# Second feed-forward matrix by seven half-size block products (Strassen) instead of eight

## The reference

```python
h = rmsnorm_2(x, mlp_norm[l])
u = jnp.square(jax.nn.relu(jnp.einsum('bsd,df->bsf', h, w_ff1[l])))   # 1024 -> 4096
x = x + jnp.einsum('bsf,fd->bsd', u, w_ff2[l])                        # 4096 -> 1024
```

## Time and profile before

| | before |
|---|---|
| median of 3 runs | 1589.47 us |
| profiled execution, its own time | 1590.67 us |
| span of that execution | 1588.9 us |
| TensorE, VectorE, ScalarE, GpSimd busy | 1547.0, 896.3, 697.8, 158.1 us |
| one feed-forward block | 87.1 us, eight of them |
| granted TensorE clock over the span | 0.997 of full speed |

### The profile page before, as it was taken

The page is one execution under the profiler, slowest core; times in us unless marked ns, Lnnn a source line. Parts: engine busy times, 40 slices in busy tenths (PEclk is TensorE's granted clock), DMA queues, the critical chain, the costliest instruction groups (busy, mean ns, idle before and its releaser), DMA issues.

```text
span 1588.9 us, 20931 instructions
## 1 busy us (share of the span) xinstructions
PE 1547.0 (97%) x7877; PEld 1263.9 (80%) x7877; DVE 896.3 (56%) x1498; ACT 697.8 (44%) x1185; POOL 158.1 (10%) x128
## 2 busy tenths in 40 slices
PE   7899999999999999999999999999999999999998
PEld 7676888877778788888888888778788888888886
DVE  5676557566866775534344345666876534344343
ACT  4355533545463774423223234563774423223232
POOL 3000222023000223000000002000223000000001
PEclk9999999999999999999999999999999999999999
DMA  5211232323211212233323232211212233233231
GB/s 171 71 33 54 80 107 80 106 95 105 80 54 62 71 55 82 95 102 107 98 87 106 79 106 89 97 52 55 66 55 91 81 106 104 89 99 106 79 106 53
DMA packets 127286, 135.62 MB, mean 85 GB/s; under 512 B 2458, under 2 KB 120804, under 8 KB 127204
## 3 DMA queue, kind: packets, MB, share of 16 engines
q1 hardware_dynamic: 126048, 133.18, 25.9%
q0 software_dynamic: 288, 1.05, 0.2%
q10 hardware_dynamic: 868, 0.31, 0.2%
HBM read 132.43 MB, written 2.10 MB: 85 GB/s over the span
## 4 chain that ended last, share of the span: by engine, by line
PE 81%; DVE 8%; ACT 4%; issue 4%; POOL 1%; DVEq 0%; ACTq 0%; POOLq 0%
PE U L1537 23%; PE U L1539 22%; PE U L1538 22%; PE U L1582 2%; PE U L1583 2%; PE U L1584 2%; PE Z L1715 1%; DVE pr L993 1%; PE Z L1730 1%; PE O L1782 1%; PE T L1755 1%; ACT tb L754 1%; PE O L1767 1%; PE Z L1641 1%; DVE WL L942 1%
## 5 line engine op out<-in xcount | busy, mean ns | idle before, releaser
L1537 PE MATMUL U<-XH,WL 128*128 128x512 f32 x976 | 386.4, 396 | 1.9 <-issue 1.9
L1539 PE MATMUL U<-XH,WH 128*128 128x512 f32 x976 | 380.5, 390 | 0.0
L1538 PE MATMUL U<-XL,WH 128*128 128x512 f32 x976 | 380.0, 389 | 0.0
L1537 PE MATMUL U<-MH,WL 128*128 128x512 f32 x848 | 336.8, 397 | 3.3 <-DVE tb L1398 1.7
L942 DVE TENSOR_TENSOR WL<-raw,WH 128x1024 fp32r<-128x1024 f32 x229 | 292.5, 1277 | 74.1 <-ACT WH L579 60.4
L579 ACT ACTIVATE WH<-raw 128x1024 fp32r<-128x1024 f32 x245 | 255.8, 1049 | 177.4 <-PE U L1539 171.1
L1539 PE MATMUL U<-MH,WH 128*128 128x512 f32 x848 | 330.6, 390 | 0.0
L1538 PE MATMUL U<-ML,WH 128*128 128x512 f32 x848 | 330.3, 389 | 0.0
L1537 PEld LDWEIGHTS U<-XH,WL 128*128 128x128 f32 x976 | 183.4, 188 | 45.0 <-issue 8.7
L1539 PEld LDWEIGHTS U<-XH,WH 128*128 128x128 f32 x976 | 183.2, 188 | 38.7
L1538 PEld LDWEIGHTS U<-XL,WH 128*128 128x128 f32 x976 | 183.6, 188 | 36.2 <-issue 0.2
(11 more groups left out here) (221 smaller groups left out, 1672.6 us busy)
## 6 DMA issues: line engine op xcount, KB each, us to landing
raw<-in_w_ff SPq DMA_DIRECT2D x64, 1024.0 KB, 5.3
raw<-in_w_in SPq DMA_DIRECT2D x24, 1024.0 KB, 5.1
raw<-in_attn_w_in SPq DMA_DIRECT2D x9, 1024.0 KB, 5.1
raw<-in_pool_w_in SPq DMA_DIRECT2D x8, 1024.0 KB, 5.4
raw<-in_w_o SPq DMA_DIRECT2D x8, 1024.0 KB, 5.0
raw<-in_attn_w_out SPq DMA_DIRECT2D x4, 1024.0 KB, 5.0
raw<-in_pool_w_out SPq DMA_DIRECT2D x4, 1024.0 KB, 4.9
xin<-in_x SPq DMA_DIRECT2D x2, 1024.0 KB, 6.4
```

The costliest lines, as they stand in the source:

```text
L1537: mm(o, wl, xh, start=first, stop=False, **kw)
L1538: mm(o, wh, xl, start=False, stop=False, **kw)
L1539: return mm(o, wh, xh, start=False, stop=last, **kw)
```

## The change

Only the second matrix changes. A pair of its output tiles (256 features), with 1024 hidden features and 512 tokens, is a product of 2 x 2 block matrices: weights in quarters (`quarters`: even or odd hidden tiles by left or right output tile), tokens in halves of 256 (B11, B21 the first halves of even and odd hidden tiles, B12, B22 the second). The variant of Strassen's scheme used makes seven products of 4 x 3 = 12 matmuls of 256 columns in place of eight. A block has four such pairs, q = 0 to 3, and a pair now is 85 matmuls: 83 of 256 columns and 2 of 512. Each engine's part:

- VectorE: four sums of weight quarters per pair (`corner_sums` 1024 wide for two of them, `third_sum`, `fourth_sum` 512 each) and their low parts (`sums_lo_of`, 1536 and 512 wide) beside the low parts of the three plain quarters (`first_halves_lo` 1024, `last_quarter_lo` 512). For the tokens, once per block: a 256-wide difference per hidden tile, two more per odd tile (`token_tile`), and per two tiles a 768-wide low part (`token_low`). The two 512-wide additions to `xT` per pair become five: `add_first` and `add_lower` 256 wide, `add_right`, `add_tops`, `add_bottoms` 512.
- ScalarE: the high parts of all these, and per pair two copies from PSUM to PSUM (`chain_copy`), which start partial sums in other banks.
- TensorE: `ff_pair`. It reads the hidden tiles k = 0, 2, 4, 6 first, then all odd ones, then the token sums. A pair may start when `add_right` of the pair before is done.
- New buffers lie over those of the attention part; `XH` of an even tile is now copied from `sq`, whose second half `token_tile` has replaced by a difference.

```diff
+                    for i in range(8):
+                        if i < 6:
                             conv(t0 + i + 2, b)
+                        elif i == 6:
+                            first_halves_hi(t0 + 8, b, (psum_done, b * 16 + (r0 + 6)))
+                            sums_hi_of(0, b, 0)
+                        else:
+                            sums_hi_of(0, b, 1)
+                            sums_hi_of(0, b, 2)
+                            last_quarter_hi(t0 + 8, b, r0 + 6)
                         if first and i == 0:
                             stat(plan["ff_stat", l])
-                        if i < 8:
-                            act.wait_ge(result_taken, b * 16 + (r0 + i + 1))
-                            a.activation(sq[:, i % 2, :], tb[:, i % 2, :], ACT.Square).then_inc(relu_squared, 1)
-                            a.activation(XH[:, i, :], tb[:, i % 2, :], ACT.Square).then_inc(second_hi_ready, 1)
-                        elif last:
-
-                            prep(G_ATTN + 8 * (l + 1) if l < DEPTH - 1 else None, i - 8, r0 + 16 * b + i, dst=MH)
+                        kp = i // 2
+                        act.wait_ge(result_taken, b * 16 + (r0 + i + 1))
+                        a.activation(sq[:, i % 2, :], tb[:, i % 2, :], ACT.Square).then_inc(relu_squared, 1)
+                        if i % 2 == 0:
+                            act.wait_ge(token_sums, b * 12 + (w0 + 3 * kp + 1))
+                            a.activation(XH[:, i, :], sq[:, 0, :], ACT.Copy).then_inc(second_hi_ready, 1)
+                        else:
+                            a.activation(XH[:, i, :], tb[:, 1, :], ACT.Square).then_inc(second_hi_ready, 1)
+                            act.wait_ge(token_sums, b * 12 + (w0 + 3 * kp + 3))
+                            a.activation(TH[:, kp, :], token_raw[:, kp, :], ACT.Copy).then_inc(token_hi, 1)
+                    for q in range(4):
+                        t = t0 + 8 + 2 * q
+                        chain_copy(q, b, 0)
+                        if q < 3:
+                            sums_hi_of(q + 1, b, 0)
+                            sums_hi_of(q + 1, b, 1)
+                            first_halves_hi(t + 2, b, (psum_done, b * 16 + (r0 + 8 + 2 * q)))
+                            chain_copy(q, b, 1)
+                            sums_hi_of(q + 1, b, 2)
+                            last_quarter_hi(t + 2, b, r0 + 8 + 2 * q)
+                        else:
+                            if not last or t + 16 * (BLOCKS - 1) + 2 < LAST_T:
+                                conv(t + 2, b)
+                            chain_copy(q, b, 1)
+                            if not last or t + 16 * (BLOCKS - 1) + 2 < LAST_T:
...
+                def chain_copy(q, b, i):
+
+                    p1, u, z, _ = strip(q)
+                    act.wait_ge(chain_done, b * 8 + (c0 + 2 * q + i + 1))
+                    if i == 0:
+                        dst, src = u, p1
+                    else:
+                        dst = z.rearrange("p (a h n) -> p a h n", a=2, h=2)[:, :, 1]
+                        src = u.unsqueeze(1).broadcast_to([P, 2, 256])
+                    a.activation(dst, src, ACT.Copy).then_inc(chain_copied, 1)
+
...
+                def corner_sums(q, b):
+
+                    t = t0 + 8 + 2 * q
+                    dve.wait_ge(raw_landed[t // 2 % 2], b * 64 + 16 * (t // 4 + 1))
+                    if q >= 2:
+                        dve.wait_ge(psum_done, b * 16 + (r0 + 8 + 2 * q - 2))
+                    shared = quarters(t)[:, 0, 1].unsqueeze(1).broadcast_to([P, 2, 4, P])
+                    out_ = sums_raw[:, q % 2, 0:1024].rearrange("p (j k c) -> p j k c", j=2, k=4)
+                    v.tensor_tensor(out_, corners(t), shared, ALU.subtract).then_inc(weight_sums, 1)
...
+                def token_tile(i, b):
+
+                    kp = i // 2
+                    c0, c1 = slice(0, 256), slice(256, 512)
+                    dve.wait_ge(relu_squared, b * 8 + (u0 + i + 1))
+                    if i % 2 == 0:
+                        v.tensor_tensor(sq[:, 0, c1], sq[:, 0, c0], sq[:, 0, c1], ALU.subtract).then_inc(token_sums, 1)
+                    else:
+                        v.tensor_tensor(token_raw[:, kp, c0], sq[:, 1, c1], sq[:, 0, c1], ALU.subtract).then_inc(token_sums, 1)
+                    dve.wait_ge(second_hi_ready, b * 8 + (m0 + i + 1))
+                    v.tensor_tensor(XL[:, i, :], sq[:, i % 2, :], XH[:, i, :].bitcast(F32), ALU.subtract).then_inc(second_ready, 1)
+                    if i % 2:
+                        dve.wait_ge(token_sums, b * 12 + (w0 + 3 * kp + 2))
+                        v.tensor_tensor(token_raw[:, kp, c1], sq[:, 1, c0], token_raw[:, kp, c0], ALU.subtract)
+                        v.scalar_tensor_tensor(out=token_raw[:, kp, 512:768], in0=token_raw[:, kp, c0], scalar=-1.0, in1=sq[:, 0, c0],
+                                               op0=ALU.mult, op1=ALU.subtract).then_inc(token_sums, 1)
+
+                def token_low(kp, b):
+
+                    dve.wait_ge(token_hi, b * 4 + (k0 + kp + 1))
+                    v.tensor_tensor(TL[:, kp, :], token_raw[:, kp, :], TH[:, kp, :].bitcast(F32), ALU.subtract).then_inc(token_lo, 1)
...
+                def add_right(q, b):
+
+                    _, _, _, e = strip(q)
+                    dve.wait_ge(fifth_done, b * 4 + (h0 + q + 1))
+                    right = xT[:, 2 * q:2 * q + 2, 256:512]
+                    v.tensor_tensor(right, right, e.unsqueeze(1).broadcast_to([P, 2, 256]), ALU.add).then_inc(half_added, 1)
...
+                    for i in range(8):
+                        if i < 6:
                             conv(t0 + i + 2, b)
+                        elif i == 6:
+                            first_halves_lo(0, b)
+                            fourth_sum(0, b)
+                        else:
+                            sums_lo_of(0, b, 0)
                         if first and i == 0:
                             stat(plan["ff_stat", l])
+                        if i in (2, 4, 6):
+                            token_low(i // 2 - 1, b)
                         ps = result(r0 + i, b)
-                        if i < 8:
-
-                            v.scalar_tensor_tensor(out=tb[:, i % 2, :], in0=ps, scalar=0.0, in1=rstd[:, 0:S], op0=ALU.max,
-                                                   op1=ALU.mult).then_inc(result_taken, 1)
-                            dve.wait_ge(relu_squared, b * 8 + (u0 + i + 1))
-                            dve.wait_ge(second_hi_ready, b * 8 + (m0 + i + 1))
-                            v.tensor_tensor(XL[:, i, :], sq[:, i % 2, :], XH[:, i, :].bitcast(F32), ALU.subtract).then_inc(second_ready, 1)
-                        else:
-                            kt = i - 8
-                            add_x(ps, kt, last, r0 + 16 * b + i if last else None)
-                            if last and l < DEPTH - 1:
-                                prep_lo(G_ATTN + 8 * (l + 1), kt, (MH, ML))
-                            elif last:
-                                v.tensor_scalar(xf[:, kt, :], xT[:, kt, :], gain[:, G_LAST + kt:G_LAST + kt + 1], None, ALU.mult).then_inc(xt_ready, 1)
+                        v.scalar_tensor_tensor(out=tb[:, i % 2, :], in0=ps, scalar=0.0, in1=rstd[:, 0:S], op0=ALU.max,
+                                               op1=ALU.mult).then_inc(result_taken, 1)
+                        if i == 5:
+                            corner_sums(0, b)
+                        token_tile(i, b)
+                        if i == 5:
+                            third_sum(0, b)
+                    sums_lo_of(0, b, 1)
+                    token_low(3, b)
+                    last_quarter_lo(0, b)
+                    for q in range(4):
+                        t = t0 + 8 + 2 * q
+                        if q < 3:
+                            corner_sums(q + 1, b)
+                        if q:
+                            add_lower(q - 1, b)
+                            add_tops(q - 1, b)
+                        if q < 3:
+                            third_sum(q + 1, b)
+                            fourth_sum(q + 1, b)
+                            sums_lo_of(q + 1, b, 0)
+                            first_halves_lo(q + 1, b)
+                        add_first(q, b)
+                        if q:
+                            add_bottoms(q - 1, b)
+                        if q < 3:
+                            sums_lo_of(q + 1, b, 1)
+                            last_quarter_lo(q + 1, b)
+                        elif not last or t + 16 * (BLOCKS - 1) + 2 < LAST_T:
+                            conv(t + 2, b)
+                            conv(t + 3, b)
+                        add_right(q, b)
+                        if last and q:
...
+                    if q >= 2:
+                        pe.wait_ge(result_taken, b * 16 + (r - 2))
+                    else:
+                        pe.wait_ge(result_taken, b * 16 + (r0 + 7))
+                    if q:
```

(28 more changed lines are left out.)

194 lines of the change are left out of this document (179 added, 15 removed).

## The result

The kernel after takes 1650.97 us, the median of 4 runs (1648.05 to 1651.53), beside 1589.33 us (1588.98 to 1591.76) for the kernel before. The ratio is 1.0379, 95% interval 1.0364 to 1.0395: slower, as forecast, and 12 us slower than the 1639 us forecast. The profiled execution took 1648.05 us with a span of 1646.2 us; that of before had 1588.9 us, so 57.3 us are to be accounted for.

A forecast was written before the change was run, and what follows sets the result against it. TensorE, busy 97% of the span, was taken as the bound, with VectorE falling late. Four blocks at +5.2 plus 2.8 a layer, two layers 47.2, +0.7 and +1.4 gave +49.3: 1639 us, with 8 in 10 from 1603 to 1666.

The forecast's parts named there:

- TensorE's gain, 0.47 us a pair: Second matrix: a pair of output tiles goes from 10.88 to 10.41 us, 14.9 us over 32 pairs.
- The first matrix falls behind: First matrix: the helpers' chain takes 11.8 us per two tiles against TensorE's 10.88; VectorE loses 0.9 us each time.
- The waits of pair 0, 7.1 us: Hand-over to the second matrix: six TensorE waits of 1.2, 1.9, 1.8, 0.9, 0.5, 0.7 us; pair 0 takes 17.5.
- So I add nothing: Hand-over: 3.4 us at half clock loses 1.7 us of matmuls, hidden by 2.1 us of waits; if later, 14 us more.
- Pairs 1 to 3 with 1.2 us of slack: Later pairs: VectorE needs 9.1 us against 10.41, so they run at TensorE's rate with 1.2 us to spare.
- Blocks of 92.3, first blocks 95.7: Feed-forward blocks: 92.3 us each, +5.2; a layer's block 0 a further +2.8 with small ends, forecast as 95.7.
- The layer change, +0.7: Between the layers: last rows of `xT` complete 1.1 and 2.2 us after TensorE's end, the norm's last sum late: +0.7 us.
- The end, +1.4: Very end: the last square starts 2.2 us after TensorE and ends at 2.9, where the norm's matmul was at 1.7: +1.4.
- From profiled to median: Whole program: the median lies 1.2 us below the profiled execution, so 1640.0 becomes 1639 us.
- The rival of the VectorE-bound pairs: Every pair: 0.1 us more on each of 12 VectorE instructions uses up the slack; 1675 us and up, chance 10%.
- the rule of the Trainium skill: VectorE: next instruction waits until the pipe is empty, 0.09 us more a step; 95.8 us a block, 1667 total, chance 3%.
- Vector keeps up: Rival in the first matrix: the waits hide and the kernel gets faster, 1577 us; chance 4%.

The follow-up runs named there:

- e5_reorder: Kernel after with the end-of-layer edits and the helpers' work in another order, each relu VectorE's first step for its tile, TensorE's order unchanged: 1605.94 us, ratio 1.0090.
- e8_small_acc: Kernel after with GpSimd's additions of the squares behind each layer's feed-forward done on 8 columns in place of 512: 1641.88 us, ratio 1.0316.
- e4_relu_early: Kernel after with the relus of tiles 6 and 7 put ahead of pair 0's weight work on VectorE: 1629.95 us, ratio 1.0243.

## Why the prediction was right, and where 12 us are missing

- **TensorE's gain, 0.47 us a pair.** Right: pairs of 10.39 and 10.40 us without idle time, and half columns cost +20.3 us for +19.7.
- **The first matrix falls behind.** Right: from the relu of tile 2 to that of tile 4 in the layer's first block, 651.99 to 663.85, are 11.86 us where 11.8 was worked out. Relus ahead of the weights take 3.1 us off the first blocks.
- **The waits of pair 0, 7.1 us; 17.5 in all.** The total is right, 17.43. The first three were 1.2, 1.9 and 1.8. The idle times of the rows are 0.98, 1.66 and 1.32; by the distance of the starts, less the 0.12 us of a matmul, it is 1.1, 1.8 and 1.8. The last three, 0.9, 0.5 and 0.7, appear only with the clock held up, as idle times of 0.70, 0.17 and 0.58 (0.9, 0.3 and 0.7 by the starts); in the kernel after the slow matmuls stand in their place. "So I add nothing" was right for the profiled execution, with little to spare: the stretch at half rate was 7 us, as the mean clock of 0.80 over 17.43 us shows, and not the 3.4 I took from the earlier trace rows. In `e5_reorder` such a stretch costs 1.5 us a block.
- **Pairs 1 to 3 with 1.2 us of slack.** Right for all blocks but a layer's last: VectorE's idle time ahead of `corner_sums` is 1.2 us in the kernel after, and 1.8 us of ballast put 0.8 to 0.9 us on a pair.
- **Blocks of 92.3, first blocks 95.7.** Right: 92.2 to 92.3, and 96.0 and 96.2. **The last block of each layer** was counted as 92.3 and is 94.1 and 93.6: the step is missing. Left out was GpSimd, which adds the squares of finished rows there and holds some of VectorE's steps up by about a us. `add_right` comes late by it, and pair 3 waits 1.45 us in one layer and 1.00 in the other. Without the wide additions these blocks take 92.3 and 92.4. 3.1 us in all.
- **The layer change, +0.7.** This is the term that was mis-sized most: +4.8. I looked at when the rows of `xT` are complete, not at what the next layer's first tile waits for. Its bank is released by `add_tops(3)`, which stands on VectorE behind `add_right(3)` and two `after_layer` steps, 2.90 us beside GpSimd. `add_tops(3)` ends at 1007.70, and TensorE starts 0.10 later. It stood still 3.2 us, and a us behind the restart the clock fell to 0.50 for 3 us, which costs about 1.5 more:

```profile
1007.03 0.67 DVE L1698 TENSOR_TENSOR xT<-xT,Z 128x512 f32<-128x512 f32 x1
```
```profile
1007.80 0.47 PE L1806 MATMUL U<-MH,WL 128*128 128x512 f32 x1 [3.03 <-issue]
```
```profile
1009.11:1012.10 2.99, 2.99 (x9) 2.32 (x7) 1.55 (x3) 2.15 (x3) 2.17 (x2) 0.50 0.00 0
```

- **The end, +1.4.** 1.6.
- **From profiled to median.** Before, the profiled execution lay 1.2 us above the median; after, 2.9 below. That is 4 of the 12 us. The longer executions of a kernel are those with the lower granted clock over the span: 0.979 with 1648.05 us and 0.976 to 0.977 with 1650.93 to 1651.53 in after, 0.983 with 1640.47 and 1640.63 and 0.978 to 0.979 with 1643.12 and 1644.14 in `e8_small_acc`. Where the half-rate stretch falls does differ from block to block, and the table of pairs 0 shows what it costs; that this is what makes one execution longer than another is argued, since only one of each kernel has a trace.

The rival of the VectorE-bound pairs was wrong as stated, at 1.2 us of slack; what I made of the rule of the Trainium skill (VectorE: DVE Perf Modes, section The DRAIN you can't avoid), 0.09 us more a step, as well, by the block of 92.2 us where it gave 95.8. "Vector keeps up" was wrong for the kernel as written, and its rival's floor too: with the sums gone altogether the kernel is still not faster than before.

## What to carry to other kernels

A change that gives the busiest engine 2% less to do is worth nothing if it takes away the distance between a result and its first use: count, for each operand, how much work lies ahead of its first reader before and after. Here 4.8 us became 1.56, and that alone ate the gain; the sums, in the order in which they were put between the helpers' steps, cost three times as much; both were mended by reordering alone. The helpers' new order (with the edits at the end of a layer) took 45 of the 61 us off, TensorE's by itself cost 27, and the two together made the kernel 0.6% faster than before. In such a walk take every engine that touches the stretch, GpSimd too, and follow for each place where work is handed on (a block's last pair, a layer's first tile) the wait that is written there, not the data it stands for.

## What the runs showed of the chip

- A VectorE step with two SBUF operands went from 0.68 to 1.78 us beside a GpSimd addition, one with a PSUM operand stayed at 0.67; GpSimd's own additions took 1.3 to 1.4 us alone and 1.3 to 1.7 in such a stretch.
- Around and behind the three waits of pair 0 (idle 0.98, 1.66 and 1.32 us) the granted clock was 0.50 for some 7 us in the kernel after, and behind one of 1.78 for 3.4 us in `e5_reorder`; behind the one wait of 2.22 us in block 1 of `e4_relu_early` it stayed at 1.00. Idle matmuls in the gap kept it at 1.00 and gave back 1.5 us a block where the matmuls behind it were ready.
- Splitting a 512-column matmul into two of 256 costs 0.014 us, 20.3 us for the 1472 split here.
